# Expert blocks of a decoder layer: down products moved behind the next block's gate and up products

## The reference

```
x = merged attention output projected + residual          # h in the kernel
u = rmsnorm(x) * g_moe
per row: best of 4 groups, best 2 of its 8 experts, two weights
rows sorted by expert, in blocks of 128 rows of one expert:
  y = (silu(u @ w_gate[e]) * (u @ w_up[e])) @ w_down[e]   # 1024x512, 1024x512, 512x1024
x = x + weight1 * y1 + weight2 * y2
out = rmsnorm(x + sigmoid(rmsnorm(x) @ w_pg) * (p @ w_pp)) * g_final
```

## Time and profile before

| | us |
|---|---|
| median of 3 runs | 2341.76 (2339.83 to 2342.63) |
| the profiled execution | 2341.29 |
| its span in the profile | 2339.7 |
| of it, experts stage (from SP's first x load to SP's first load of `finish`) | 1472.1 to 2162.9 |
| TensorE busy over the span | 1979.1 (85%) |
| VectorE, ScalarE, GpSimd busy | 1173.8, 855.4, 281.2 |

### The profile page before, as it was taken

The page is one execution under the profiler, slowest core; times in us unless marked ns, Lnnn a source line. Parts: engine busy times, 40 slices in busy tenths (PEclk is TensorE's granted clock), DMA queues, the critical chain, the costliest instruction groups (busy, mean ns, idle before and its releaser), DMA issues. The chain is left out here.

```text
span 2339.7 us, 27599 instructions
## 1 busy us (share of the span) xinstructions
PE 1979.1 (85%) x10140; PEld 1528.1 (65%) x10140; DVE 1173.8 (50%) x1355; ACT 855.4 (37%) x1171; POOL 281.2 (12%) x356
## 2 busy tenths in 40 slices
PE   5999999698898799991488992599999999997598
PEld 5999999687777667770286541466666666664485
DVE  5121212188888645443342224466666666664664
ACT  4111111166666334440031000444444444442454
POOL 0110101143333200001021003000000000000210
PEclk7999999899999969895689995799999999999699
DMA  3444343434121222207244003999999999993520
GB/s 110 116 132 120 108 126 113 140 114 145 46 73 46 58 51 41 41 1 196 72 156 145 28 18 140 340 373 354 352 363 350 345 352 355 359 350 148 199 99 37
DMA packets 222237, 392.70 MB, mean 168 GB/s; under 512 B 29467, under 2 KB 100619, under 8 KB 222164
## 3 DMA queue, kind: packets, MB, share of 16 engines
q1 hardware_dynamic: 202916, 325.28, 40.9%
q0 software_dynamic: 14928, 50.60, 6.8%
q10 hardware_dynamic: 4320, 15.85, 1.7%
HBM read 321.02 MB, written 78.35 MB: 171 GB/s over the span
## 5 line engine op out<-in xcount | busy, mean ns | idle before, releaser
L1825 PE MATMUL x_Y<-x_wd,x_hT 128*128 128x512 f32 x512 | 228.1, 598 | 32.4 <-DVE x_hT L1918 32.4
L86 PE MATMUL p_acc<-uh,p_wl 128*128 128x344 f32 x720 | 235.1, 327 | 12.8 <-DVE ul L292 8.6
L88 PE MATMUL p_acc<-uh,p_wh 128*128 128x344 f32 x720 | 230.7, 320 | 0.0
L87 PE MATMUL p_acc<-ul,p_wh 128*128 128x344 f32 x720 | 230.6, 320 | 0.0
L304 DVE COPY p_zk<-p_tp 128x512 f32<-128x512 f32 (+1 forms) x90 | 44.2, 547 | 304.5 <-PE p_tp L225 304.5
L1825 PEld LDWEIGHTS x_Y<-x_wd,x_hT 128*128 128x128 f32 x512 | 94.6, 190 | 147.0 <-issue 147.0
L1903 DVE TENSOR_TENSOR x_wgl<-x_wg,x_wgh 128x2048 fp32r<-128x2048 f32 x64 | 146.4, 2287 | 69.7 <-ACT x_wgh L1856 69.7
L268 ACT ACTIVATE p_zc<-p_acc 128x344 f32<-128x344 f32 x90 | 41.2, 458 | 321.7 <-PE p_acc L88 321.7
L86 PEld LDWEIGHTS p_acc<-uh,p_wl 128*128 128x128 f32 x720 | 135.9, 189 | 17.8 <-issue 15.0
L1903 DVE TENSOR_TENSOR x_wul<-x_wu,x_wuh 128x2048 fp32r<-128x2048 f32 x64 | 143.6, 2285 | 0.0
L544 PE MATMUL g_acc<-uh,g_wl 128*128 128x344 f32 x384 | 131.8, 343 | 9.1 <-ACT u L575 7.0
(11 more groups left out here) (317 smaller groups left out, 4062.0 us busy)
## 6 DMA issues: line engine op xcount, KB each, us to landing
x_wg<-in_w_gate SPq DMA_DIRECT2D x64, 1024.0 KB, 7.2
x_wu<-in_w_up SPq DMA_DIRECT2D x64, 1024.0 KB, 7.1
x_wd<-in_w_down SPq DMA_DIRECT2D x32, 2048.0 KB, 12.1
x_x<-xs SPq DMA_DIRECT2D x32, 512.0 KB, 9.8
ys<-x_y POOLq DMA_DIRECT2D x32, 512.0 KB, 5.5
zT<-p_zc ACTq DMA_DIRECT2D x30, 516.0 KB, 3.5
p_w<-in_w_in SPq DMA_DIRECT2D x30, 512.0 KB, 5.5
ztok<-p_zk POOLq DMA_DIRECT2D x30, 512.0 KB, 4.6
```

The lines of the kernel that those rows point to most:

```text
L86: pe.matmul(out, w_low, m_high, start=first, stop=False)
L87: pe.matmul(out, w_high, m_low, start=False, stop=False)
L88: return pe.matmul(out, w_high, m_high, start=False, stop=last)
L1825: last = pe.matmul(Y[c][:, :], hT[:, k, :], wd[:, b, k, c * 512:(c + 1) * 512], start=(k == 0), stop=(k == KF - 1))
```

## The change

- TensorE, in the step that brings in block m: gate of m-1, transposes of hm of m-2, up of m-1, transposes of x of m, down of m-2. The down products run k outside and the two output halves inside, and one semaphore (`d_used`) tells of all eight. The first two passes are written out (`PEEL = 2`); the last step has both remaining blocks' down products.
- VectorE and ScalarE follow: `hT` of m-2 is copied right after `gs` of m-1, both low parts of the gate weights come before `hm` and the scaling of x; ScalarE copies Y of m-3 at the start of the step and now also issues the store to `ys`.
- SP requests the down weights of block m-1 after the up weights of block m.
- Rows are dealt to partitions as (p k) instead of (k p) for x, hm, the gains and the three weights: partition p holds 8 (for down 4) successive input rows, so that a weight load is one contiguous run a partition. The transposes of x read columns 8 floats apart, those of hm 4 apart.
- `h` is a tile of `residual`, which stores it to `h_kept` in DRAM tile by tile; `finish` has an `h` of its own and loads it: tiles 0 and 1 beside the first tiles of p, tiles 2 to 8 after the weights and ahead of `gf`.

```
-        Wg = g["w_gate"].rearrange("a e (k p) f -> (a e) p k f", p=P)
+        Wg = g["w_gate"].rearrange("a e (p k) f -> (a e) p k f", p=P)
...
-                need(sp, y_full, it * 4 + (2 * b - 2))
-                sp.dma_start(wd[:, b, :, :], w(Wd)).then_inc(d_in[b], 16)
+                one = lag(it, b, 1)
+                if one:
+                    load_down(*one)
...
+                by_k = x[:, b, :].rearrange("t (p k) -> t k p", k=KD)
...
-                        last = pe.transpose(tpx[c][:, k, :], x[:, b, (c * 4 + k) * P:(c * 4 + k + 1) * P], ident[:, :])
+                        last = pe.transpose(tpx[c][:, k, :], by_k[:, c * 4 + k, :], ident[:, :])
...
             def step(it, j):
-                behind = j or not isinstance(it, int)
-                p_, b, n = (it, 0, it * 2) if j else (it - 1, 1, it * 2 - 1)
-                if behind:
-                    gate_up(n)
-                turn(it, j)
-                if behind:
-                    down(p_, b, n)
+                one, two = lag(it, j, 1), lag(it, j, 2)
+                if one:
+                    gate(one[0])
+                if two:
+                    turn_hidden(two[0])
+                if one:
+                    up(one[0])
+                turn(it * 2 + j, j, it)
+                if two:
+                    down(*two)
...
+                row = act.value_load(meta_row[0:1, bass.ds(n * 4 + 1, 1)], min_val=0, max_val=ASG)
+                act.dma_start(ys[bass.ds(row, P), :], y[:, b, :]).then_inc(y_out[b], 16)
...
             def step(it, j):
-                if behind:
-                    gated(n)
-                low(new, 0, wg, wgh, wgl, gh_full, gl_full)
-                if behind:
-                    hidden(n)
-                    hidden_T(n)
-                turn(new)
-                low(new, 1, wg, wgh, wgl, gh_full, gl_full)
+                if one:
+                    gated(one[0])
+                if two:
+                    hidden_T(two[0])
+                for half in range(2):
+                    low(new, half, wg, wgh, wgl, gh_full, gl_full)
+                if one:
+                    hidden(one[0])
+                turn(new)
                 low_x(new)
                 for half in range(2):
                     low(new, half, wu, wuh, wul, uh_full, ul_full)
...
+            for t in range(2, TT):
+                load_h(t)
             sp.dma_start(gf[:, :], g["g_final"].unsqueeze(0).broadcast_to([P, D])).then_inc(gf_in, 16)
```

More of the change, by code:

```diff
@@ L50 @@
 MAXBLK = (ASG + NE * (P - 1)) // P
+MINPAIR = (-(-ASG // P) + 1) // 2
 NEG = -1.0e30
@@ L1444, in _ @@
                 sp.dma_start(xt[0:rows(t), t % 2, :], x_of(t)).then_inc(x_in[t % 2], 16)
+                if t >= 2:
+                    sp.dma_start(g["h_kept"][(t - 2) * P:(t - 1) * P, :], h[:, t - 2, :]).then_inc(h_out, 16)
+            for t in range(TT - 2, TT):
+                sp.wait_ge(h_full, t + 1)
+                sp.dma_start(g["h_kept"][t * P:t * P + rows(t), :], h[0:rows(t), t, :]).then_inc(h_out, 16)
+            sp.wait_ge(h_out, 16 * TT)
         @block.tensor
@@ L1751, in experts @@
         block = ctx.enter_context(nc.Block())
-        def pairs(eng):
-            return eng.value_load(meta_row[0:1, 2:3], min_val=(-(-ASG // P) + 1) // 2 - 1,
-                                  max_val=(MAXBLK + 1) // 2 - 1) + 1
+        PEEL = 2
         def passes(eng, step, end):
[L1761 to L1764, removed]
+            n = eng.value_load(meta_row[0:1, 2:3], min_val=0, max_val=(MAXBLK + 1) // 2 - MINPAIR) + MINPAIR
+            for it in range(PEEL):
+                for j in range(2):
+                    step(it, j)
+            with eng.Fori(PEEL, n) as it:
@@ L1768, in passes, with lag @@
                 end(n)
+        def lag(it, j, back):
+            new = it * 2 + j
+            if isinstance(it, int) and new < back:
+                return None
+            return new - back, (j - back) % 2, it + (j - back) // 2
         @block.sync
@@ L1792, in _, with end, turn @@
+            def end(np_):
+                load_down(np_ * 2 - 1, 1, np_ - 1)
+            passes(sp, step, end)
         @block.tensor
         def _(pe):
-            def turn(it, b):
+            def turn(new, b, it):
                 pe.wait_ge(x_in[b], it * 16 + 16)
+                by_k = x[:, b, :].rearrange("t (p k) -> t k p", k=KD)
                 for c in range(2):
-                    need(pe, xT_full, it * 4 + (2 * b + c - 1))
+                    need(pe, xT_full, new * 2 + (c - 1))
@@ L1799, in turn, with gate_or_up @@
                     for k in range(4):
-                        last = pe.transpose(tpx[c][:, k, :], x[:, b, (c * 4 + k) * P:(c * 4 + k + 1) * P], ident[:, :])
+                        last = pe.transpose(tpx[c][:, k, :], by_k[:, c * 4 + k, :], ident[:, :])
                     last.then_inc(tpx_full, 1)
-            def gate_up(n):
+            def gate_or_up(n, bank, wh, wl, cut, full):
+                for k in range(KD):
+                    if k % 4 == 0:
+                        pe.wait_ge(cut, n * 2 + (k // 4 + 1))
+                    last = products(pe, bank[:, :], xh[:, k, :], xl[:, k, :], wh[:, k, :], wl[:, k, :],
+                                    k == 0, k == KD - 1)
+                last.then_inc(full, 1)
@@ L1805, in gate_up, with gate, up @@
+            def gate(n):
                 pe.wait_ge(xl_full, n + 1)
+                need(pe, gs_full, n)
+                gate_or_up(n, G, wgh, wgl, gl_full, g_full)
+            def up(n):
                 need(pe, hm_full, n)
[L1807 to L1812, removed]
@@ L1842, in _ @@
+                if two:
[5 more added lines that the diff above has]
+                    down(*two)
+            def end(np_):
+                last = np_ * 2 - 1
+                gate(last)
+                turn_hidden(last - 1)
+                up(last)
+                down(last - 1, 0, np_ - 1)
+                turn_hidden(last)
+                down(last, 1, np_ - 1)
             passes(pe, step, end)
@@ L1935, in end @@
             def end(np_):
-                gated(np_ * 2 - 1)
-                hidden(np_ * 2 - 1)
-                hidden_T(np_ * 2 - 1)
+                last = np_ * 2 - 1
+                gated(last)
+                hidden_T(last - 1)
+                hidden(last)
+                hidden_T(last)
             passes(dve, step, end)
@@ L1971, in finish @@
         C = D // 2
+        h = sb("h", [P, TT, D])
+        hs_in = [sem(f"h_in{t}") for t in range(TT)]
         wpgh, wpgl = (sb(n, [P, KD, D], F32R) for n in ("wpgh", "wpgl"))
```

113 lines of the change are left out of this document (59 added, 54 removed).

## The result

| us | before | changed |
|---|---|---|
| first comparison, median (lowest to highest) | 2340.95 (2339.83 to 2342.63, 4 runs) | 2319.55 (2309.26 to 2322.21, 4 runs) |
| the same again, later | 2349.88 (2339.16 to 2370.83, 23 runs) | 2319.33 (2316.65 to 2325.23, 6 runs) |
| profiled execution, span | 2339.7 | 2320.6 |

What follows compares the result with a forecast made beforehand. TensorE's order was taken to bound the experts stage, with DMA next. Terms -35.0 + 1.9 + 5.4 + 1.0 - 1.5 + 5.5 + 1.0 = -21.7 us took 2341.3 to 2319.6 us; range 2310 to 2350.

Steps and rivals of the forecast that it cites:

- The steady block: Experts stage: TensorE's wait for hT goes, 1.10 us a block, 20.9 to 19.8; with the last block -35.0 us.
- the rest stays as it is: Steady experts block: gate and up keep their 11.6 us and the down products their 6.57 us.
- The start: Start of experts: first gate later +1.9 us, TensorE gap before second gate +5.4, lower clock afterwards +1.0.
- lower clock after it: Second gate of experts, after TensorE's gap: between 0 and 1.8 us longer, taken as +1.0.
- The gains in `finish`: Seven h loads ahead in SP's queue make the gains land 4.9 us late; with queue gaps +5.5 us.
- The end and the start of `finish`: Last y store lands sooner, -1.5 us; two h tiles share DMA with finish's first gather, +1.0 us.
- The issue on ScalarE: Experts block: issuing the y store takes ScalarE about 1.5 us where it idles, so costs nothing.
- The layout: Experts weight loads and transposes of x and hm from strided columns: 0 us taken, at most 44.6 in all.
- Rival 1: Experts blocks: strided transposes cost as much as at half clock, 44.6 us more, total 2364.2; chance 0.18.
- The sign of being wrong that I had named: Transposes in experts: weight loads longer than the present 140 ns would show the forecast wrong.
- Rival 2: Experts blocks: DMA stays at 353 GB/s and bounds, block 20.8 us, total 2354; chance 0.07.
- Rival 3: Steady experts blocks: VectorE's chain, under 2 us of cover, runs late; half the gain goes, about 2337; chance 0.10.

Runs made afterwards that it cites:

- hidden_late: Changed kernel with hidden transposes back right in front of the down products: 2417.43 us with VectorE doing xT before hT, 2353.15 us in the other run with hT first.
- gains_first: Changed kernel with the load of the final gains ahead of the seven h loads in finish; ratio to the kernel before 0.9814.
- h_sbuf: Changed kernel with h kept in SBUF from residual to finish, without h stores or loads; ratio to the kernel before 0.9823.

## Why the prediction was off

- **The steady block** is the step that failed, by its size. Mechanism right: the wait for hT goes, nothing takes its place. But the gain was sized too small: said 1.10 us a block and 35.0 in all; measured 20.82 - 19.42 = 1.40 a block. The stage's change of -35.8 (means of two profiles) less the +8.3 of its start leaves -44.1 us, 31 x 1.42. The missing 0.3 has three parts. From the hidden transposes to the down products it was 1.67 us on average over the 32 blocks, and I had put the 1.62 of one block; in the new place they cost 0.39 + 0.08 (up takes that much longer), not 0.52: together 1.20. The x transposes ahead of the next instruction took 0.98 and now 0.89; they do so with the wait back too (both hidden_late runs), so this tenth comes with the rewritten step and not with the wait, and what in it makes it stays open. Down, from a standstill, 6.57 and now 6.47. I had taken "the rest stays as it is" and one block for all, without the restart of the down products behind the wait.
- **The start** was right: first gate +1.6 (said 1.9), gap 4.83 beyond the transposes (5.4), lower clock after it +1.1 and +2.3 in the two profiles (1.0, bound 1.8: exceeded once). With 0.2 for the first gate's own length that is 8.3, as said.
- **The gains in `finish`** cost 7.2 us, not 5.5: the second term mis-sized. Their lateness of 5.24 us is as worked out (4.9 and gaps). The other 2.0 is the clock after the wait, which I had priced at the start of experts and put at nothing here. TensorE stood idle for 5.19 us (6.27 in the second profile) and then took eight transposes and the first products at the lower clock, granted 0.59, where gains_first has 1.00. From the rows that is some 1.5 us by estimate: the transposes 0.6 longer, the first products another 0.9. All of it hangs on this load.
- **The end and the start of `finish`**: said -1.5 and +1.0, measured -0.2 in the sum of both. One profile puts the store's move at 1.8, h_sbuf puts h's first tiles at under 1, both within the 1.9 us by which two profiles of the kernel before differ there. The issue on ScalarE, put at about 1.5 us and then at nothing, takes 0.34 in the trace.
- **The layout**: 0 taken, 1.4 us measured over the stage, some 4 ns a transpose. Rival 1 fell. The Trainium skill (SBUF — State Buffer, Door 1: The DMA port swizzle) says that reading is at full rate only while accesses hit a 16-byte line more than once, and that spoke for it; the trace shows no such price for the time of these transposes. The sign of being wrong that I had named, weight loads longer than 140 ns, did come (192 ns) and was no sign: the transposes' rhythm has room for it. Whether 16-byte lines are what lengthens these records no run tells.
- **Rival 2** (DMA at 353 GB/s) fell: the rate followed demand, 353, 379, 424. **Rival 3** did not come: its chain ended in time in every steady block. I had priced it too low: in hidden_late a wait of about 2 us in each block came back for another reason, and the time was 98 us above the changed kernel's, where I gave this rival half of the gain.
- **The comparison**: I held 0.2% to be what a measurement tells, on three runs within 2.8 us. The kernel before spreads over 32 us in 23 runs, 1.3%. The low end of my range, 2310, was set against one profile with the dilated stage at its shortest.

In sum: -44.1 + 8.3 + 7.2 - 0.2 at the seam is -28.8, where -35.0 + 8.3 + 5.5 - 0.5 = -21.7 stood.

## What to carry to other kernels

Price a wait by the whole stretch between the instructions before and behind it, averaged over all its occurrences, and not by the idle time of one; and look at what runs behind it, since TensorE's next work can be at the lower clock (behind 5.19 us of idle time in `finish`, behind most waits of 1.84 and 2.12 us in hidden_late). When data moves to DRAM to free space, look at what stands behind its loads in the queue; one small load that is needed first belongs ahead of them. And compare kernels stage by stage before believing that two totals agree.

## What was not expected of the hardware

- TensorE waits of 1.84 and 2.12 us in turn, one a block, were followed in 21 of 30 blocks by products at the lower clock (granted 0.94 over that stage, down 8.26 instead of 6.57 us), waits of 0.78 to 1.1 us in none (down 6.57 in every block). One wait a block, in the same place, made blocks of 20.6 us or of up to 23.5.
- One unchanged stage took 206.8, 212.7 or 218.1 us, never anything between, in 14 profiles: three lengths some 5.6 us apart, with a granted clock of 0.87, 0.84 or 0.82. What picks the length in a run stays open.
- 424 GB/s over 300 us by one core with TensorE, VectorE and ScalarE all at work.
